# The last expert's results added by TensorE instead of being stored and fetched, its preceding down product moved up, and the shares formed later

## What is computed

```python
aff = sigmoid(h @ router_w)
sel_group = argmax(sum of the two best of aff + router_b, per group)
_, idx = top_k(where(in_group, biased, -inf), 2)
wts = sel_aff / sum(sel_aff)
for e in range(16):
    he = silu(h @ w_gate[e]) * (h @ w_up[e])
    y = y + combine[..., e:e + 1] * (he @ w_down[e])
x_l = x_l + mod_l[5] * y_l
```

## Time and profile before

| | |
|---|---|
| median of 3 runs | 986.45 us (984.69 to 990.89) |
| the profiled execution | 985.22 us, of which the span is 983.4 us |
| PE busy | 809.0 us, 82% |
| DVE busy | 386.5 us, 39% |
| ACT busy | 181.1 us, 18% |
| POOL busy | 37.8 us, 4% |
| DMA | 320.56 MB, mean 326 GB/s |

### The profile page before, as it was taken

How to read it: one execution, slowest core, us unless ns; L and a number is a source line. 1 busy time by engine, 2 the same in 40 slices (tenths; PEclk the granted TensorE clock), 3 DMA queues, 4 the chain that set the end, 5 groups by cost and what they waited for, 6 DMA issues and landing times.

```text
span 983.4 us, 18044 instructions
## 1 busy us (share of the span) xinstructions
PE 809.0 (82%) x6896; PEld 434.7 (44%) x6897; DVE 386.5 (39%) x882; ACT 181.1 (18%) x389; POOL 37.8 (4%) x63
## 2 busy tenths in 40 slices
PE   8899899997979677887759977799779969697590
PEld 3544646444544334543325533374345535254250
DVE  3267879858978741211001211333512111121113
ACT  3221010326530201111010110330211111111101
POOL 0000000120001010000000000100100000000001
PEclk9799999999989788998879988899979989798786
DMA  9899977999406897779999899893979999999944
GB/s 343 294 357 353 327 261 278 344 340 328 159 1 238 359 358 295 290 281 417 416 417 415 338 416 356 309 408 120 386 278 374 393 413 416 415 416 414 418 157 144
DMA packets 102858, 320.56 MB, mean 326 GB/s; under 512 B 12960, under 2 KB 28192, under 8 KB 86304
## 3 DMA queue, kind: packets, MB, share of 16 engines
q1 hardware_dynamic: 78448, 282.84, 73.5%
q0 software_dynamic: 4592, 21.41, 5.9%
q10 hardware_dynamic: 19776, 15.75, 4.9%
HBM read 303.58 MB, written 24.64 MB: 334 GB/s over the span
## 4 chain that ended last, share of the span: by engine, by line
issue 29%; PE 28%; DMA 14%; DVE 13%; SPq 11%; ACT 2%; ACTq 1%; POOL 1%; POOLq 0%; DVEq 0%
PE bank L1474 7%; SPq L476 6%; DMA raw<-in_w_up 5%; DMA arena<-unit_rows 4%; PE bank L1695 4%; PE bank L1804 3%; SPq L445 2%; DMA ring<-in_w_in 2%; PE bank L1478 2%; PE bank L1410 2%; PE bank L1708 2%; DVE bias L885 2%; PE bank L1483 1%; PE bank L1767 1%; SPq L461 1%
## 5 line engine op out<-in xcount | busy, mean ns | idle before, releaser
L1695 PE MATMUL bank<-raw,arena 128*32 128x256 f32 x3392 | 251.8, 437 | 78.8 <-DMA raw<-in_w_up 44.9
L1695 PEld LDWEIGHTS bank<-raw,arena 128*32 128x32 f32 x3392 | 121.4, 123 | 187.4 <-DMA raw<-in_w_up 60.5
L1291 DVE TENSOR_TENSOR arena<-arena,bank 64x256 f32<-64x256 f32 x53 | 22.5, 424 | 349.4 <-ACT arena L794 349.4
L1708 PE MATMUL bank<-raw,arena 128*32 128x256 f32 x1696 | 115.0, 395 | 0.8 <-DVE arena L1279 0.8
L1708 PEld LDWEIGHTS bank<-raw,arena 128*32 128x32 f32 x1696 | 61.9, 116 | 41.7 <-issue 7.0
L1474 PE MATMUL bank<-ring,arena 128*128 128x512 f32 x160 | 70.0, 595 | 0.2 <-DMA ring<-in_w_in 0.2
L885 DVE SCALAR_TENSOR_TENSOR bias<-ring,small,bias 128x512 f32<-128x512 f32 x84 | 63.2, 752 | 3.0
L794 ACT ACTIVATE arena<-bank 64x256 f32<-64x256 f32 x53 | 19.9, 375 | 238.0 <-PE bank L1695 212.7
L1682 PE MATMUL bank<-consts_sb,arena 64*128 64x64 f32 x212 | 35.6, 289 | 23.4 <-DVE arena L1291 19.4
L1474 PEld LDWEIGHTS bank<-ring,arena 128*128 128x128 f32 x160 | 30.1, 190 | 38.3 <-issue 37.2
L1410 PE MATMUL bank<-consts_sb 128*128 128x512 f32 x88 | 46.9, 681 | 0.0
(11 more groups left out here) (239 smaller groups left out, 806.0 us busy)
## 6 DMA issues: line engine op xcount, KB each, us to landing
raw<-in_w_gate SPq DMA_DIRECT2D x64, 1024.0 KB, 19.5
raw<-in_w_up SPq DMA_DIRECT2D x64, 1024.0 KB, 21.0
raw<-in_w_down SPq DMA_DIRECT2D x64, 1024.0 KB, 22.4
ring<-in_ada_w SPq DMA_DIRECT2D x24, 2048.0 KB, 13.1
ring<-in_w_in SPq DMA_DIRECT2D x7, 2048.0 KB, 14.7
unit_results<-arena ACTq DMA_DIRECT2D x244, 32.0 KB, 7.1
arena<-unit_rows ACTq DMA_DIRECT2D x55, 128.0 KB, 6.9
ring<-in_w_out SPq DMA_DIRECT2D x2, 2048.0 KB, 42.4
```

Source lines behind the costliest of these rows:

```text
L1695: ins = mm(ps[4][o:o + S, 0:FW], xT[:, i, j * S:(j + 1) * S], w[:, k % 4, h * FW:(h + 1) * FW], start=(k == 0), stop=(k == KD - 1))
L1708: ins = mm(ps[5][j * S:(j + 1) * S, 0:XW], hT_e[:, k % QN, k // QN * S:(k // QN + 1) * S], w[:, k % 2, j * XW:(j + 1) * XW], start=(k == 0 ...
```

## The change

The units of the last expert position (15) are no longer stored and fetched. VectorE writes each unit's result to `ys`, and eight matmuls (`scatter`) add it to PSUM banks 0 to 3, cleared before: the stationary operand `late_T` (32 rows of a 128-row table for each bank) holds each token's share where the token is in this unit. `weigh` takes the last expert's share out of `share` and keeps it apart; `late_diagonals`, one 128x512 matmul and `late_row` build the table between positions 13 and 15. POOL waits only for the stores of the other experts. VectorE adds the fetched rows and then the four banks to `xl`. For position 15 TensorE runs `down` of the unit before ahead of `gate_up`. The loop of rounds is one round shorter, and positions 13 to 15 are written out. The shares are formed after the first unit's rows are turned. SP fetches the modulation rows from `expert_begun` 16 on; the first four modulation sums are issued ahead of the last `scatter`, two of their copies on ACT are moved between the squares of the norm, and the twelve idle-filling matmuls there (2, 8 and 2) become seven (2, 3 and 2). The last part of layer 1's modulation goes to a buffer of its own (`third`), and two half-buffers of layer 1 are loaded after six instead of eight linear-map groups. Not shown in the diff are those two, one new column of constants, one more filled row block, and the loop bounds.

```diff
-MODS_FIRST = 8
+MODS_FIRST = 4
...
-        y_of = (f_, lay([("second", (TT, D))], 2 * D)[0]["second"])
+        y_of = ([f_[:, t, :] for t in range(TT)], [bias[:].rearrange("p a n -> p (a n)"), arena[:, 3 * D:4 * D]])
...
-            sp.wait_ge(L[0]["expert_closed"], NE - 1)
+            sp.wait_ge(L[0]["expert_begun"], NE)
...
+                if s < NH:
+                    sp.wait_ge(L[0]["expert_closed"], NE)
...
+                    sp.wait_ge(mix_ps, 6)
+                if s == 2 * FNET_AT + 2:
                     sp.wait_ge(mix_ps, 8)
...
-                pool.wait_ge(all_stored, l + 1)
+                pool.wait_ge(further_stored, l + 1)
+                pool.wait_ge(L[l]["y_stored0"], (NE // 2) * 16 * JN)
+                pool.wait_ge(L[l]["y_stored1"], (NE // 2 + 1) * 16 * JN)
...
+                    if k == 3 and t:
+                        for n in range(MODS_FIRST, MODS_FIRST + 2):
+                            mod1_copy(n)
...
+                n_tok = act.value_load(cnt_i[0:1, NE - 1:NE], min_val=0, max_val=SEQ)
                 act.wait_ge(E["y_stored2"], act.snap(odd, min_val=1, max_val=MAX_UNITS) * (16 * JN))
                 act.wait_ge(E["y_stored3"], act.snap(even, min_val=1, max_val=MAX_UNITS) * (16 * JN))
-                nc.scalar.copy(s_done[:, l:l + 1], ssq[:, 0:1]).then_inc(all_stored, 1)
+                nc.scalar.copy(s_done[:, l:l + 1], ident[:, 0:1]).then_inc(further_stored, 1)
+                n = act.snap(units, min_val=NE - 1, max_val=MAX_UNITS)
+                store_y(n, n * S, 1)
+                late_unit()
+                with act.If(n_tok > S):
+                    with act.Fori(S, n_tok, S):
...
+            def weigh():
+
+                aff, t16, u16, o1, o2, s1 = (rt[n] for n in ("aff", "t16", "u16", "o1", "o2", "s1"))
+                link(nc.vector.tensor_tensor(u16, t16, aff, ALU.mult))
+                link(nc.vector.reduce_sum(s1[:, :, 6:7], u16, axis=AX))
+                link(nc.vector.reciprocal(s1[:, :, 7:8], s1[:, :, 6:7]))
+                link(nc.vector.tensor_tensor(comb, u16, s1[:, :, 7:8].to_broadcast([P, TT, NE]), ALU.mult))
+                nc.vector.tensor_copy(rel, ps[6][:, 0:TT * NE].rearrange("p (t e) -> p t e", t=TT)[:, :, NE - 1:NE])
+                link(nc.vector.tensor_copy(late_share, comb[:, :, NE - 1:NE]))
+                link(nc.vector.memset(comb[:, :, NE - 1:NE], 0.0))
+                for q, o in enumerate((o1, o2)):
+                    link(nc.vector.tensor_tensor(picked, o, comb, ALU.mult))
+                    link(nc.vector.reduce_sum(share[:, :, q:q + 1], picked, axis=AX))
...
+                def late_weights():
+
+                    nc.vector.scalar_tensor_tensor(late_T, late_rows[:, 0:SEQ], late_at, late_rows[:, SEQ:2 * SEQ],
+                                                   ALU.is_equal, ALU.mult).then_inc(late_ready, 1)
+
+                def late_diagonals():
+
+                    for b in range(2):
+                        dve.wait_ge(acc_saved[b], 16 * (N_ADA // 2))
+                    for b, cols in enumerate((rel, late_share)):
+                        for t in range(TT):
+                            at = (TT * b + t) * P
+                            ins = nc.vector.tensor_scalar(bias[:, 0, at:at + P], ident, cols[:, t, :], None, ALU.mult)
+                    ins.then_inc(late_diag, 1)
+
+                def late_row():
+
+                    dve.wait_ge(late_in_psum, l + 1)
+                    nc.vector.tensor_copy(late_at, cst("lane")).then_inc(late_ready, 1)
+                    link(nc.vector.tensor_copy(late_rows, ps[2][:]))
+                    for b in range(3):
+                        nc.vector.memset(ps[b][:], 0.0)
+                    link(nc.vector.memset(ps[3][:], 0.0))
+                    late_weights()
...
+                n_tok = dve.value_load(cnt_i[0:1, NE - 1:NE], min_val=0, max_val=SEQ)
+                n = dve.snap(units, min_val=1, max_val=MAX_UNITS)
+                turn_back(n - 1)
+                result(n - 1, 1, NE // 2)
+                product(n)
+                turned(n + 1)
+                dve.reg_add(units, units, 1)
+                dve.wait_ge(E["y_stored0"], (NE // 2) * 16 * JN)
+
+                def late_result(n):
+
+                    dve.wait_ge(E["y_in_psum"], n + 1)
+                    nc.vector.tensor_tensor(ys[:, 0, :], ps[5][:, 0:XW], gate_s, ALU.mult).then_inc(E["y_ready"], 1)
...
                 n = dve.snap(units, min_val=NE, max_val=MAX_UNITS)
                 turn_back(n - 1)
-                result(n - 1, 0, NE // 2)
-
-            def combine_results(l):
-
+                add_fetched(l, 0)
+                late_result(n - 1)
+                add_fetched(l, 1)
+                dve.wait_ge(scattered, dve.snap(late, min_val=1, max_val=2 * UN))
+                dve.reg_add(late, late, 1)
                 for t in range(TT):
-                    dve.wait_ge(y_back[t], 32 * (l + 1))
-                    for q in range(2):
-                        ins = nc.vector.scalar_tensor_tensor(xl[:, t, :], y_of[q][:, t, :], share[:, t, q:q + 1],
-                                                             xl[:, t, :], ALU.mult, ALU.add)
-                        if q == 0:
-                            link(ins)
+                    for j in range(JN):
+                        part = xl[:, t, j * XW:(j + 1) * XW]
+                        ins = nc.vector.tensor_tensor(part, part, ps[j][:, t * XW:(t + 1) * XW], ALU.add)
                     ins.then_inc(added, 1)
+
+            def add_fetched(l, t):
+
+                dve.wait_ge(y_back[t], 32 * (l + 1))
+                for q in range(2):
+                    link(nc.vector.scalar_tensor_tensor(xl[:, t, :], y_of[q][t], share[:, t, q:q + 1],
+                                                        xl[:, t, :], ALU.mult, ALU.add))
...
+                def scatter(n, last):
+
+                    m = pe.snap(late, min_val=1, max_val=2 * UN)
+                    pe.wait_ge(E["y_ready"], n + 2)
+                    pe.wait_ge(late_ready, m * 2)
+                    for t in range(TT):
+                        for j in range(JN):
+                            ins = mm(ps[j][:, t * XW:(t + 1) * XW], late_T[j * S:(j + 1) * S, t * P:(t + 1) * P],
+                                     ys[j * S:(j + 1) * S, 0, :], start=False, stop=False, skip_group_check=True)
+                            if last and (t, j) == (0, 0):
+                                ins.then_inc(E["expert_closed"], 1)
+                    ins.then_inc(scattered, 1)
+                    pe.reg_add(late, late, 1)
...
+                    if i == NE - 3:
+                        pe.wait_ge(late_diag, l + 1)
+                        mm(ps[2][:], ones, bias[:, 0, :], start=True, stop=True).then_inc(late_in_psum, 1)
+                    further(n_tok, own)
...
+                prev, own = own, held((NE - 1) % HELD, (NE - 1) // HELD)
+                n_tok = pe.value_load(cnt_i[0:1, NE - 1:NE], min_val=0, max_val=SEQ)
+                n = pe.snap(units, min_val=1, max_val=MAX_UNITS)
+                turn_he(n - 1)
+                down(n - 1, prev)
+                gate_up(n, own, True)
+                turn_x(n + 1, True)
+                pe.reg_add(units, units, 1)
+                with pe.If(n_tok > S):
+                    with pe.Fori(S, n_tok, S):
+                        n = pe.snap(units, min_val=1, max_val=MAX_UNITS)
+                        turn_he(n - 1)
+                        gate_up(n, own, False)
+                        down(n - 1, own)
+                        turn_x(n + 1, False)
+                        scatter(n - 1, False)
+                        pe.reg_add(units, units, 1)
                 n = pe.snap(units, min_val=NE, max_val=MAX_UNITS)
                 turn_he(n - 1)
-                down(n - 1, held((NE - 1) % HELD, (NE - 1) // HELD))
-
-            experts(0)
+                down(n - 1, own)
+                if l == 0:
+                    for k in range(MODS_FIRST):
+                        sum_mod1(k)
+                scatter(n - 1, True)
 
             def sum_mod1(n):
...
             keep_busy(2, 4)
-            for n in range(N_ADA):
+            for n in range(MODS_FIRST, N_ADA):
+                if n == MODS_FIRST + 2:
+                    keep_busy(3, 4)
                 sum_mod1(n)
-                if n == MODS_FIRST - 1:
-                    keep_busy(8, 4)
             keep_busy(2, 4)
 
             pe.wait_ge(dft_in, 16)
```

117 lines of the change are left out of this document (79 added, 38 removed).

## The result

Eight runs of the changed kernel have a median of 974.25 us (971.17 to 979.94), eight of the kernel before, on the same chip, 986.18 (982.60 to 990.89). The ratio is 0.988 with a 95% interval of 0.986 to 0.991: a gain of 12 us, where 18 were forecast (968). The gain is real, over 1%, and two thirds of the size. The profiled execution has a span of 975.1 against 983.4; it was 2.6 us above its own median. A second profile of the same kernel, which the experiments begin with, has 972.9.

What follows compares the result with a forecast made beforehand. TensorE waits for weights; the change touches only both layers' ends, round trips through DRAM. 985.2 - 10.3 (layer 0) - 0.7 (shares) - 7.7 (layer 1) = 966.5; median 1.2 above, so 968; own range 963 to 972, wide 962 to 976.

Steps and rivals of the forecast that it cites:

- Layer 0's -10.3: End of layer 0: the last addition ends at 623.9 instead of 634.2, a gain of 10.3 us.
- a store lands 5.8 after its issue: Layer 0, position 14's stores: issued by 600.8, landed at 606.0 to 606.6, so POOL fetches at about 606.5, against 621.99.
- the middle of the free and the in-step case: Layer 0's fetch beside the modulation fetch: second pair back at 617.8, between 616.1 undisturbed and 619.5 with queues advancing together.
- The Fourier matmuls start 9.65 after the last addition: Behind layer 0's additions: norm and sums keep their relation, so the Fourier matmuls follow by 9.65 us as before.
- The shares' -0.7: Forming the shares, both layers: moving eight VectorE instructions away gains 0.35 us a layer, 0.7 in all.
- Layer 1's -7.7: End of layer 1: the last addition ends at 969.0 instead of 976.7, a gain of 7.7 us.
- The +1.4 for each round: Layer 1's two loop rounds: each adds 0.3 us of waiting for the late result and 1.1 of scatter.
- contention: Rival, layer 0: the fetch comes last of all transfers, the gain there is 4.8 us, time 973; chance 0.09.
- The clock: Rival: TensorE's clock is at its lower level through the Fourier stage, making the change slower, up to 998; chance 0.04.
- Serial scatter: Rival: scatter's matmuls run one after the other, 3.5 us each instead of 1.1, time 974; chance 0.08.
- nothing gained: Rival: the fetch starts no earlier because POOL's wait on position 14's stores is late, time 990; chance 0.05.
- the one on the second pair: Sign, layer 0's fetch: the forecast is wrong if the second pair of rows is back after 620.

Runs made afterwards that it cites:

- sums8: Changed kernel with eight instead of four of the twelve modulation sums ahead of the scatter in TensorE's order; median 971.33 us.
- store_first: Changed kernel with position 14's result stored ahead of ScalarE's last count load and its waits on the further units' stores; median 974.35 us.
- mods_late: Changed kernel with only SyncE's modulation fetch back at its old, later place (asked for at 608.51 instead of 600.6); median 976.31 us.
- mods_split: Changed kernel with only the first 1 MB modulation part asked for early, the other two and the Fourier table after the fetched results; median 972.04 us.
- best: Changed kernel with two modulation parts early, the third and the Fourier table behind the fetch, and eight sums ahead of the scatter; median 971.98 us.

## Why the prediction was right in sign and short in size

The direction held, and so did the path through the fetch, the additions and the norm. 974.25 lies in the wide range (962 to 976) but outside the forecast's own (963 to 972): the upper end had been drawn over two rivals. The largest term was mis-sized. **Layer 0's -10.3** came out as -3.6 at the last addition and -2.6 at the Fourier matmuls. By its own steps, with the last addition 6.7 late against 623.9:

- *"result 598.3".* 600.67, so +2.4: position 14's product stood 2.5 later in this execution (595.18 for 592.68), by its weights. In sums8 it was 599.08.
- *"a store lands 5.8 after its issue", fetch at 606.5.* The fetch began 10.4 after the result where I had 8.2: +2.2. I thought of issue and landing as two fixed lengths. store_first shows that an earlier issue gains 0.2 of 1.1, and mods_late that it isn't the modulation. What sets the 10.4 beyond that is not shown. The median of 5.8 mixes four stores beneath weight loads with eight on emptier DMA engines.
- *"the middle of the free and the in-step case".* The fetch took 14.0, not 11.3: +2.7. mods_split (at most 9.7 with 1 MB beside it), best (12.5 with 2 MB) and the changed kernel (14.0 with 3.5 MB) show the fetch stretched by what is beside it. The DMA engines moved 374 to 420 GB/s from 606 to 622, where before they had fallen to 21. I had the rule and split the difference. The in-step case was nearer: 1.7 of the 2.7. It fits the Trainium skill's sentence that transfers of different issuing engines interleave (DMA: Bandwidth & Descriptors, section Issuing engines are not separate DMA queues).
- *The additions.* 2.73 for eight, not 3.4: -0.7. Scatter, 1.15, and VectorE's order held.
- *"The Fourier matmuls start 9.65 after the last addition".* 10.6: +1.0. I argued that TensorE's filling showed it to have slack. The fillers stand in its queue in order, and the sums behind them wait; already before, the start stood 2.2 behind the norm, 3.2 after. sums8 brought that to 0.15.

**The shares' -0.7** came out as -0.15. VectorE's step from the last member (351.55 before, 351.42 after) to the ranks took 1.99 in layer 0, where it was 2.00 (353.55 - 351.55), and 1.64 in layer 1, where it was 1.78. The forecast took the ranks to be ready at 353.1 because their matmuls' rows ended there, but without the shares ahead of it VectorE still waits for that bank until 353.41, 0.46 behind the end of those rows (351.66 + 1.29):

```profile
353.41 0.29 DVE L1275 TENSOR_TENSOR arena<-bank,consts_sb 128x128 f32<-128x128 f32 x1 [1.80 <-PE bank L1762]
```

**Layer 1's -7.7** came out as -7.2, and that is luck: three errors nearly cancel. The first interval took 7.42, not 5.6. The next `gate_up` did start 1.7 closer behind the product, but ran at half clock and took 5.41 where I had 3.66. In the kernel before, the same spell of half clock lay under the `down` that was moved, and its 7.33 held 1.0 of it, so at equal clock the move was worth 1.1 and not 1.7. And where the clock is full, the fetch that the move brought forward into the late positions takes 1.3 to 3.0 instead (6.5 to 8.2 against 5.20), which no rival named. Against that, the last `down` followed the third product after 4.0, not 4.5, and the last addition ended 8.3 behind that `down`, not 9. The +1.4 for each round was right (7.67 against 6.34 before). In the mark "17.5 behind the first late product" I had counted from the product's end; from its start it is 17.9, and 19.1 was measured.

Of the **rivals**, contention was the true one. The fetch took 14.0 where that rival's would take 16.8 (623.3 - 606.5), but it began 4.6 later than either had it, so the last addition came at 630.6, behind the rival's 629.4, and the time is nearer to its 973 than to 968. The clock did halve (0.50 from 936 to 945, where 1.00 is full) and cost 2.2 in the first interval, where it had cost 1.0 before, but nothing at the Fourier stage, where the rival had it. Serial scatter and "nothing gained" did not occur; between positions 13 and 15 VectorE ended no wait but the 0.8 for the hidden rows' copy, which the moved product follows by its nature, and the table's work lay in idle time (7.34 idle ahead of the next product in layer 1). Of my marks, the one on the second pair says that the forecast is wrong: it came back after 620. The fetch at 606.5, the last addition at 624 and the 9.65 behind it were missed as well.

## What to carry to other kernels

When a change lets a transfer start earlier, price it with everything that will then be moving, and ask whether an idle stretch of the DMA engines was what made the old lengths short: here the gain of starting 11 us earlier was cut by 4.3 of stretching and by stores that land with the backlog, not with their issue. Test a pair of edits apart before trusting either: the additions alone gave 5, the move alone nothing, both 12. Compare steps at the same granted clock and in the same layer: a part that one trace ran at half clock makes a move look worth more than it is. And filler work on an in-order engine is not slack; look whether the first real work behind it is started by its input or by the filler's end.
